# Four heads a round instead of two in the attention of a fused two-block layer

## What is computed

```python
# first block: groups g = 0, 1, 2 with (window, dilation) = (128,1), (512,4), (2048,16)
scores = einsum('bdhnqe,bdhnke->bdhnqk', qb, kb) * e ** -0.5   # blocks of 128 queries
scores = where(mask, scores, NEG_INF)
m = max(scores, axis=-1)
p = exp(scores - m[..., None])
den = sum(p, axis=-1)
o = einsum('bdhnqk,bdhnke->bdhnqe', p, vb) / den[..., None]
# the three groups are combined with weights den * exp(m - max over groups)
# second block: one more attention with a window of 128 and a sink logit in the softmax
s = einsum('bnqhgd,bnkhd->bnhgqk', qb, kk) * scale
p = softmax(concatenate([where(valid, s, NEG_INF), sink]))[..., :-1]
o = einsum('bnhgqk,bnkhd->bnqhgd', p, vv)
```

## Time and profile before

| | |
|---|---|
| median of 3 runs | 2779.8 us (2776.28 to 2780.31) |
| the profiled execution | 2781.19 us, of it span 2779.4 us |
| mean granted TensorE clock | 0.98 of full speed |
| TensorE matmul busy | 2642.9 us, 12424 instructions |
| VectorE busy | 1397.6 us, 2486 instructions |
| ScalarE busy | 616.2 us, 1361 instructions |
| GpSimd busy | 893.0 us, 870 instructions |
| attention 0 | about 211 to 410 us |
| attention 1 | about 559 to 751 us |
| attention 2 | about 904 to 1081 us |
| attention 3 | about 1610 to 1860 us |

### The profile page before, as it was taken

One profiled execution on the slowest core, in us unless ns is written; L12 is line 12 of the kernel. 1 busy time (PEld: TensorE's weight loads), 2 busy tenths in 40 slices (PEclk: granted clock), 3 DMA queues, 4 the chain that ended last, 5 costly groups with the idle time before them and its releaser, 6 DMA issues.

```text
span 2779.4 us, 33376 instructions
## 1 busy us (share of the span) xinstructions
PE 2642.9 (95%) x12424; PEld 2183.5 (79%) x12424; DVE 1397.6 (50%) x2486; ACT 616.2 (22%) x1361; POOL 893.0 (32%) x870
## 2 busy tenths in 40 slices
PE   6999999999999998959999899989999999999997
PEld 5787779977899776748788767768778888888886
DVE  5611449977687774671563611133373433434336
ACT  3213321123211323430122033330141010110102
POOL 3422223422333231314334322224223333333333
PEclk8999999999999999989999899999999999999999
DMA  7311221222311233534342022225241111111113
GB/s 234 97 46 50 65 72 39 64 69 77 116 39 62 75 105 114 189 118 143 108 136 90 24 84 69 69 87 164 75 148 50 47 52 52 45 45 45 53 60 121
DMA packets 153637, 236.05 MB, mean 85 GB/s; under 512 B 22818, under 2 KB 67618, under 8 KB 153508
## 3 DMA queue, kind: packets, MB, share of 16 engines
q1 hardware_dynamic: 152356, 230.14, 26.2%
q10 hardware_dynamic: 1152, 4.19, 0.4%
HBM read 181.65 MB, written 52.63 MB: 84 GB/s over the span
## 4 chain that ended last, share of the span: by engine, by line
PE 80%; DVE 13%; DMA 4%; issue 1%; ACT 1%; POOL 1%; SPq 0%; POOLq 0%; DVEq 0%; ACTq 0%
PE ps L1825 47%; PE ps L2017 12%; PE ps L2049 12%; DVE scr L1384 4%; PE ps L1935 3%; PE ps L1911 2%; PE ps L1921 2%; PE ps L1854 1%; DMA small<-st_d 1%; DMA scr<-in_x 1%; DVE act_lo L1257 1%; DVE scr L1499 1%; DVE scr L1277 0%; POOL w_lo L896 0%; DVE scr L1364 0%
## 5 line engine op out<-in xcount | busy, mean ns | idle before, releaser
L894 POOL CAST w_hi<-raw 128x512 fp32r<-128x512 f32 x416 | 303.1, 729 | 1819.1 <-DMA raw<-in_w_in 870.7
L896 POOL TENSOR_TENSOR w_lo<-raw,w_hi 128x512 fp32r<-128x512 f32 x416 | 578.5, 1391 | 33.3
L1825 PE MATMUL ps<-act_hi,w_hi 128*128 128x512 f32 x1344 | 549.8, 409 | 38.9 <-DVE act_lo L1257 36.6
L1825 PE MATMUL ps<-act_lo,w_hi 128*128 128x512 f32 x1344 | 548.2, 408 | 0.0
L1825 PE MATMUL ps<-act_hi,w_lo 128*128 128x512 f32 x1344 | 530.0, 394 | 0.0
L1384 DVE SCALAR_TENSOR_TENSOR scr<-scr,small 128x512 f32<-128x512 f32 x480 | 429.0, 894 | 14.3
L1825 PE MATMUL ps<-w_hi,act_hi 128*128 128x512 f32 (+1 forms) x960 | 388.3, 404 | 13.5 <-DVE act_lo L1257 11.1
L1825 PE MATMUL ps<-w_lo,act_hi 128*128 128x512 f32 (+1 forms) x960 | 377.4, 393 | 0.0
L1825 PE MATMUL ps<-w_hi,act_lo 128*128 128x512 f32 (+1 forms) x960 | 377.3, 393 | 0.0
L1825 PEld LDWEIGHTS ps<-act_hi,w_hi 128*128 128x128 f32 x1344 | 256.1, 191 | 92.0 <-issue 48.3
L1825 PEld LDWEIGHTS ps<-act_lo,w_hi 128*128 128x128 f32 x1344 | 254.4, 189 | 69.3 <-issue 14.6
(11 more groups left out here) (185 smaller groups left out, 2821.9 us busy)
## 6 DMA issues: line engine op xcount, KB each, us to landing
raw<-in_w_in SPq DMA_DIRECT2D x176, 256.0 KB, 3.2
raw<-in_w_up SPq DMA_DIRECT2D x64, 256.0 KB, 2.7
raw<-in_w_down SPq DMA_DIRECT2D x64, 256.0 KB, 2.6
vreg<-in_w_ada SPq DMA_DIRECT2D x48, 256.0 KB, 3.9
raw<-in_w_in SPq DMA_DIRECT2D x72, 128.0 KB, 2.4
x_d<-big SPq DMA_DIRECT2D x16, 512.0 KB, 3.1
scr<-x_d SPq DMA_DIRECT2D x16, 512.0 KB, 4.3
o_d<-scr SPq DMA_DIRECT2D x48, 128.0 KB, 2.1
```

The costliest lines, as they stand in the source:

```text
L894: pool.tensor_copy(dhi, src).then_inc(w_hi_done, 1)
L896: pool.tensor_tensor(dlo, src, dhi.bitcast(F32), ALU.subtract).then_inc(w_ready, 1)
L1825: ins = nc.tensor.matmul(out_, lhs, rhs, start=(m == 0), stop=(m == 3 * nk - 1))
```

## The change

Two pairs become one round of four heads (r = 0 to 15 in place of p = 0 to 31). Bank `ps_s[j]` holds the scores of heads j of both pairs (e = 0, 1), 256 columns each; the transposes are written back into the same bank, and ScalarE's copy back into `prob[j]`, now 512 columns wide. `ps_t` and `probT` are gone. The output copy takes 256 columns for four heads. The waits follow: scores wait for both copies out of the banks, reductions for the third and fourth score matmul and for the value matmuls of the round before, transposes and value matmuls bank by bank. The projection matmuls of a round are 36 (48 in attention 3): 6, 20 and 10 (8, 27 and 13) in place of twice 2, 12 and 4 (twice 3, 15 and 6). VectorE runs the taps of four head steps together at the end of the round. The attention's 64 steps on SyncE are as before but for the counts that it waits on.

```diff
-def pair_fill(C, p):
-    per = att_share(C)
-    a, b = 2 * p * per, 2 * p * per + 2 * per
-    return a, a + 2 * per // 8, b - 2 * per // 4, b
+def four_fill(C, r):
+    n = 4 * att_share(C)
+    a = r * n
+    return a, a + n // 6, a + n - 5 * n // 18, a + n
...
-        prob = [scr[:, i * 256:(i + 1) * 256] for i in range(2)]
-        probT = scr[:, 512:1024]
+        prob = [scr[:, i * HALF:(i + 1) * HALF] for i in range(2)]
...
+            def probs_out(g, r, j):
+                n = att_cfg(g, r // 2)[1]
+                act.wait_ge(probs_t, 32 * g + 2 * r + j + 1)
+                both = lambda t: t.rearrange("p (e k) -> p e k", e=2)[:, :, 0:n]
+                nc.scalar.activation(both(prob[j]), both(ps_s[j]), ACT.Copy).then_inc(pt_out, 1)
...
+            def att_four(g, r):
                 us = att_units(g)
+                a, b, c, d = four_fill(len(ATT_STAGES[g]), r)
                 for i in units_in(a, b):
                     f_unit(us[i])
                 for j in range(2):
+                    for e in range(2):
+                        exps(g, r, j, e)
                 for i in units_in(b, c):
                     f_unit(us[i])
-                probs_out(g, p)
+                for j in range(2):
+                    probs_out(g, r, j)
                 for i in units_in(c, d):
                     f_unit(us[i])
...
+            def score_max(g, r, j, e):
+                B, h = r // 2, pair_heads(g, 2 * r + e)[j]
                 _, n, mask = att_cfg(g, B)
+                dve.wait_ge(scores, 64 * g + 4 * r + 3 + j)
+                if 16 * g + r >= 1:
+                    dve.wait_ge(pv, 16 * g + r)
+                nc.vector.tensor_tensor_reduce(prob[j][:, 256 * e:256 * e + n], ps_s[j][:, 256 * e:256 * e + n], mask,
+                                               -0.125, c_ns[:, h:h + 1] if g == 3 else 1e30, ALU.add, ALU.min,
                                                stat[:, B, h:h + 1]).then_inc(att_max, 1)
...
+                nc.vector.tensor_copy(obuf[quad % 2], src).then_inc(o_out, 1)
...
+                for r in range(16):
+                    a, b, c, d = four_fill(C, r)
                     for i in units_in(a, b):
                         f_unit(us[i])
+                    if r >= 1:
+                        out_four(g, r - 1)
                     for j in range(2):
-                        score_max(g, p, j)
+                        for e in range(2):
+                            score_max(g, r, j, e)
                     for i in units_in(b, d):
                         f_unit(us[i])
-                    conv_taps(("step", g, 2 * p))
-                    conv_taps(("step", g, 2 * p + 1))
-                out_pair(g, 31)
+                    for n in range(4):
+                        conv_taps(("step", g, 4 * r + n))
+                out_four(g, 15)
...
+            def score_four(g, r):
+                B = r // 2
                 k0, n, _ = att_cfg(g, B)
+                if 16 * g + r >= 1:
+                    pe.wait_ge(pt_out, 32 * g + 2 * r)
+                for e in range(2):
+                    i = (2 * r + e) % 4
+                    for j in range(2):
+                        rows = slice(64 * j, 64 * j + 64)
+                        keys = kT[rows, i, k0:k0 + n] if g < 3 else kT2[rows, k0:k0 + n]
+                        nc.tensor.matmul(ps_s[j][:, 256 * e:256 * e + n], qT[rows, i, P * B:P * B + P], keys,
+                                         start=True, stop=True).then_inc(scores, 1)
+
+            def turn_four(g, r):
+                n = att_cfg(g, r // 2)[1]
                 for j in range(2):
+                    pe.wait_ge(probs, 64 * g + 4 * r + 2 * j + 2)
+                    for e in range(2):
+                        for i in range(n // P):
+                            cols = slice(256 * e + P * i, 256 * e + P * i + P)
+                            ins = nc.tensor.transpose(ps_s[j][:, cols], prob[j][:, cols], ident[:, :])
+                    ins.then_inc(probs_t, 1)
+
+            def value_four(g, r):
+                k0, n, _ = att_cfg(g, r // 2)
+                if 16 * g + r >= 1:
+                    pe.wait_ge(o_out, 16 * g + r)
                 for j in range(2):
+                    pe.wait_ge(pt_out, 32 * g + 2 * r + j + 1)
+                    for e in range(2):
+                        h = pair_heads(g, 2 * r + e)[j]
+                        for i in range(n // P):
+                            v = (V[:, k0 // P + i, 64 * h:64 * h + 64] if g < 3
+                                 else V2[:, k0 // P + i, 64 * (h // 4):64 * (h // 4) + 64])
+                            ins = nc.tensor.matmul(ps_o[:, P * e + HD * j:P * e + HD * j + HD],
+                                                   prob[j][:, 256 * e + P * i:256 * e + P * i + P], v, start=(i == 0),
+                                                   stop=(i == n // P - 1))
                 ins.then_inc(pv, 1)
```

More of the change, by code:

```diff
@@ L628, in store_heads @@
                 a = 64 * g + s
-                sp.wait_ge(o_out, a // 2 + 1)
+                sp.wait_ge(o_out, a // 4 + 1)
                 k = (a // 4) % 2
@@ L715, in _ @@
                     wait_stored(sp, ("za", t, h))
-            sp.wait_ge(pv, 32 * NG)
+            sp.wait_ge(pv, 16 * NG)
             conv_block(0)
@@ L1066, in _ @@
                     qkv_unit(u)
-                for p in range(32):
-                    att_pair(g, p)
+                for r in range(16):
+                    att_four(g, r)
             def ln_root(B):
@@ L1165, in _ @@
                                      scale=c_ps[:, u[1]:u[1] + 1]).then_inc(free_of(u), 1)
[L1166 to L1169, removed]
+            for r in range(16):
+                att_four(3, r)
+                if r % 2 == 0 and r:
+                    act.wait_ge(y2_den, r // 2)
                     nc.scalar.activation(tiny[:, 8:16], tiny[:, 0:8], ACT.Exp).then_inc(y2_exp, 1)
@@ L1682, in y2_weights @@
                 nc.vector.tensor_tensor(tiny[:, 0:8], stat[:, B, 0:8], c_ns, ALU.subtract).then_inc(y2_den, 1)
-            for p in range(32):
-                if p >= 1:
-                    out_pair(3, p - 1)
+            for r in range(16):
+                if r >= 1:
+                    out_four(3, r - 1)
                 for j in range(2):
[L1688 to L1693, removed]
+                    for e in range(2):
+                        score_max(3, r, j, e)
+                if r % 2 == 0 and r:
+                    y2_weights(r // 2 - 1)
+                if r % 2 == 1 and r > 1:
+                    y2_scale(r // 2 - 1)
+            out_four(3, 15)
             y2_weights(7)
@@ L1901, in qkv_unit @@
                     project(u)
-            def score_pair(g, p):
-                B = p // 4
+            def score_four(g, r):
+                B = r // 2
                 k0, n, _ = att_cfg(g, B)
-                if 32 * g + p >= 1:
-                    pe.wait_ge(att_max, 64 * g + 2 * p)
-                for j in range(2):
[L1909 to L1918, removed]
-                for j in range(2):
[L1920 to L1936, removed]
-                                               stop=(i == n // P - 1))
+                if 16 * g + r >= 1:
+                    pe.wait_ge(pt_out, 32 * g + 2 * r)
```

66 lines of the change are left out of this document (22 added, 44 removed).

## The result

The changed kernel takes 2747.3 us (median of 4 runs, 2745.6 to 2752.7) against 2780.1 us (median of 4, 2776.3 to 2782.0): ratio 0.9885, 95% interval 0.9872 to 0.9899, so 33 us or 1.15% faster. The forecast was 19 us. The profiled execution took 2745.55 us, of it span 2743.8.

The account below looks back on a forecast made before the run. TensorE, busy 95% of the span, was taken to bound the kernel. Score visits 12.8, waits 4.4 and clock 1.9 sum to 19.1 us saved, giving 2760.7 us; range 2750 to 2774.

Parts of the forecast that it names:

- the slower side: Rival, score matmuls: the two heads stop running side by side, fully lost costing 70 us, 2830 us; chance 0.07.
- The price of a visit: Scores on TensorE: changing to 64 rows and back costs about 0.20 us; 64 fewer visits save 12.8 us.
- loads hidden in the longer group: Rival, scores: the second pair's weight loads slide under the first pair's streaming, 12.8 us more saved, 2748 us; chance 0.05.
- Transposes and values: On TensorE: nothing fixed per group, four transposes 0.44 us, eight value matmuls 0.92 us; merging them saves 0.
- Waits: Transposes in the four attentions wait for ScalarE's exponentials 7.7 us instead of 12.1, saving 4.4 us.
- Taps beside GpSimd: Rival, VectorE's eight-tap blocks: taps run at 1.12 us each, 12 us lost in all, 2773 us; chance 0.12.
- The clock: Attention 3's start: with 1.4 us of wait for 5.1, the loss at the 1.2 GHz level is won back, 1.9 us.

## Why the prediction was wrong

**Direction and bound: right.** TensorE was the bound, the gain lay in fewer visits to the scores plus a few waits, and no rival came near the slower side.

**The price of a visit: the step that failed.** The prediction read 0.09 + 0.10 at the edges as the whole change of rows, and ascribed the other 0.10 in each of the two score steps to a weight load in the open, which the second pair would pay again with its own 0.64 or 0.42. It is not paid again. In the changed kernel the four steps of a score group at 256 keys are 0.32, 0.22, 0.22 and 0.31 us; the middle two carry nothing beyond their columns (0.11 per 128 columns, twice). At 128 keys they are 0.21, 0.11, 0.11 and 0.21. So the term was 64 x 0.40 = 25.6 us instead of 12.8. The rival "loads hidden in the longer group" had this price right and a chance of 0.05. Its 2748 is the time that came, in part by luck: the ordinary rounds gave 3.4 us more than the 25.6, and the clock 3.0 less than the 1.9 that it shares with the forecast (both below). And its name is only half the mechanism: the run with scores over 128 rows shows that the 0.10 in the outer steps too exist only where the rows change. Today's group of one pair had just two steps, both of them edges; the prediction took what both steps show for what every step would show. The kernel before could not tell these apart, and the chance should have been nearer to even.

By the Trainium skill, page "TensorEngine Tiling (Array Packing)", "Key Properties", a change of tiling mode drains TensorE. The trace agrees in so far as it has a fixed cost at the changes and nowhere else: 0.40 us for there and back at 64 rows, nothing at 128. The rule of the Trainium skill that the prediction weighed, page "TensorE: Matmul & The Clock Gate", Part 3, "The mechanism" (weight loads pulled ahead), agrees with the inner steps, and the trace bears it out.

**Transposes and values: nearly right.** Eight transposes cost 0.79 (275.13 to 275.92) + 0.09 = 0.88, twice 0.44. Sixteen value matmuls cost 1.70 + 0.08 = 1.78 where twice 0.92 was foreseen: 0.06 a round, some 2 us in all. The run with values in two groups shows no fixed price (12.21 again), so this small gain stays unexplained.

**Waits: right.** 8.4 us against 7.7 foreseen; by attention 0 + 2.6 + 3.5 + 2.3 against 0 + 2.9 + 3.4 + 1.4. None at the start of attention 1. The mechanism (gate, eight taps, copy, reductions) is what the rows show, and moving the taps removed it.

**Taps beside GpSimd: a real effect in the wrong place.** In attention 2's late rounds they ran at 0.78. At 1.13 on average they ran in attention 1 when the reductions stood ahead of them, where it costs nothing: there a tap beside nothing took 0.75 us, and two that began during a 1.6 us subtraction of GpSimd took 1.67.

**The clock: a step left out.** The loss in attention 3 did come back: around its wait of 1.96 us the granted clock stays at 1.00, the 2.4 GHz level. It was undersized, 1.9 for 2.3: half the clock over 4.60 us loses 2.3, and the spacing of the scores says the same, for the first two pairs of attention 3 took 20.99 us with a wait of 5.10 in them, the next two 13.61, which leaves 2.3. But the clock now falls behind the late round of attention 1 and behind one of the two in attention 2, where it was full before. The changed kernel, windows (us, busy and counts for PE, PEld, DVE, ACT, POOL, then the granted clock):

```profile
602.00:606.40 4.40, 2.16 (x11) 1.46 (x10) 4.29 (x14) 1.01 (x5) 1.40 (x2) 1.00 0.77 261
606.40:607.80 1.40, 1.07 (x5) 0.83 (x6) 1.36 (x2) 1.38 (x6) 1.40 (x2) 0.58 0.67 176
607.80:611.20 3.40, 3.40 (x13) 2.67 (x12) 3.29 (x4) 0.38 (x1) 3.24 (x4) 0.67 0.24 87
...
1020.00:1023.20 3.20, 1.46 (x8) 0.80 (x7) 1.69 (x10) 2.11 (x10) 0.00 (x0) 0.98 0.36 92
1023.20:1026.50 3.30, 3.30 (x10) 2.56 (x9) 3.18 (x4) 0.55 (x3) 2.37 (x2) 0.50 0.57 177
...
1590.00:1620.00 30.00, 27.71 (x140) 21.94 (x139) 4.88 (x27) 8.29 (x29) 10.67 (x12) 1.00 0.42 131
```

In attention 2 TensorE stood still for 1.41 us ahead of the fall, then ran four transposes with another stop of 0.33 between them; behind it 3.3 us hold 10 matmuls at 0.50, the 1.2 GHz level. In attention 1 it stood still for 2.24 us and the clock fell about when the first two transposes ran. The prediction counted the waits of these rounds and no clock behind them. From these rows: 1.40 x 0.42 + 3.40 x 0.33 = 1.7 us in attention 1 and 3.30 x 0.50 = 1.65 in attention 2, 3.4 together, more than the 2.3 won in attention 3.

Whether a stop costs clock is not fixed by its length. The first excerpt is the second late round of attention 2 in the same trace, with the stops of the first (1.40 and 0.33) and full clock behind them; the second is the start of attention 3 in the run with the heads in series:

```profile
1046.61 0.44 PE L1923 MATMUL ps<-ident,scr 128*128 128x128 f32 x2 [1.40 <-ACT scr L1038]
...
1047.50:1051.00 3.50, 3.50 (x21) 3.08 (x22) 2.10 (x3) 0.84 (x3) 0.00 (x0) 1.00 0.04 17
```

```profile
1603.12 1.46 PE L1923 MATMUL ps<-ident,scr 128*128 128x128 f32 x4 [1.95 <-ACT scr L1038]
...
1603.20:1606.60 3.40, 3.29 (x10) 2.41 (x11) 0.00 (x0) 1.80 (x7) 2.81 (x3) 0.50 0.39 108
```

The two late rounds of attention 2 took 14.18 and 12.60 us from scores to scores: that 1.6 us is what the fallen clock alone cost. With the heads in series the clock fell behind all four late turns (the two rounds then took 14.26 and 14.19); with the scores in two visits it fell behind none. So the clock's part in a single total, here and in the sum below, is partly luck. What decides it no run here tells.

**The sum.** Foreseen: 12.8 + 4.4 + 1.9 = 19.1. Found in the attentions: 29.0 in the ordinary rounds (25.6 by visits, 2.2 by values, 1.2 not ascribed), 3.7 in the waits, 2.3 - 3.4 = -1.1 for the clock: 31.6 of 34.5 us. The remaining 2.9 are not ascribed.

## What to carry to other kernels

Where a few matmuls over part of the rows stand between matmuls over all of them, count the visits and not the matmuls: each visit costs a fixed time at its ends (0.40 us here), and merging two of them saves it whole, while cutting the group of value matmuls over 128 rows cost nothing. A cost that shows in every step of a group of two may belong to its ends; before pricing "twice as much of it", look for a longer group or bound it both ways with even chances. And when work is gathered into longer blocks on a side engine, look at what stands behind the block in the rounds in which its input is late: putting the urgent reductions ahead of the block was worth another 10 us in the attentions, the clock's part included.

## What the hardware showed

- The two halves of the array take their own instructions as they come: with the heads in series in the queue the eight score instructions took 1.08 us, with the heads alternating 1.07. In both traces the matmuls of the two halves start in pairs within 15 ns, although with the heads in series four of one half are queued ahead of the first of the other. (In the records the two passes without a signal come first, then the two with one. They don't name the half; that a pair is one of each follows from the time, for eight such passes one behind the other took 1.54 us in the run over 128 rows.) The Trainium skill, page "TensorE: Matmul & The Clock Gate", Part 3, "The mechanism", has matmuls start strictly in program order; across the halves this trace shows them otherwise.
- Going to 64 rows and back costs 0.40 us, in four steps of about 0.10 each, at 128 and at 256 keys alike (measured with both halves in use).
- TensorE's granted clock fell to 0.50 for 3.3 us behind a stop of only 1.41 + 0.33 us (attention 2), and stayed at 1.00 behind one of 1.96 + 0.33 (attention 3) and behind one of 1.40 + 0.33 (attention 2 again). A wait of some 2 us cost up to 1.7 us more behind it, or nothing.
- Eight taps of VectorE took 6.26 us in one place and 9.07 in another, 0.78 and, beside GpSimd's subtractions, 1.13 each on average (0.75 to 1.67).
